# Order of the first loads and warm products at the start, and a router with tokens stationary on the turned residual stream

## The reference, cut to what matters

```python
hf = rms_norm(x, norm_ffn[layer])
...
logits = (h @ w_router).astype(jnp.float32) + b_router.astype(jnp.float32)
top_val, top_idx = lax.top_k(logits, TOP_K_EXPERTS)
top_w = jax.nn.softmax(top_val, axis=-1)
...
for e in range(N_EXPERTS):
    out = out + gates[..., e:e + 1] * swiglu(h, w_gu[e], w_down[e])
```

## Time and profile before

| | us |
|---|---|
| median of 3 runs (1910.8 to 1911.77) | 1911.51 |
| profiled execution | 1911.39 |
| its span | 1909.0 |
| TensorE busy | 1881.3 |
| VectorE, ScalarE busy | 1503.9, 1269.9 |

### The profile page before, as it was taken

One profiled execution on the slowest core, in us unless ns is written; L12 is line 12 of the kernel. 1 busy time (PEld: TensorE's weight loads), 2 busy tenths in 40 slices (PEclk: granted clock), 3 DMA queues, 4 the chain that ended last, 5 costly groups with the idle time before them and its releaser, 6 DMA issues.

```text
span 1909.0 us, 27543 instructions
## 1 busy us (share of the span) xinstructions
PE 1881.3 (99%) x9439; PEld 1581.3 (83%) x9439; DVE 1503.9 (79%) x1670; ACT 1269.9 (67%) x1689; POOL 86.6 (5%) x125
## 2 busy tenths in 40 slices
PE   7999999999999999999999999999999999999998
PEld 6887898888888887898788888888888888888886
DVE  4888664645456898665699999999999999999998
ACT  5747543544444747554578888888888788887885
POOL 1020000000000020001220000000000000000000
PEclk9999999999999999999999999999999999999999
DMA  9454653765554453564399999999999999999995
GB/s 341 136 187 133 213 188 132 260 204 194 196 176 139 132 189 123 193 215 137 115 394 404 382 395 352 409 380 371 392 357 407 376 375 384 364 406 377 377 406 199
DMA packets 182590, 530.17 MB, mean 278 GB/s; under 512 B 8896, under 2 KB 18176, under 8 KB 182256
## 3 DMA queue, kind: packets, MB, share of 16 engines
q1 hardware_dynamic: 175136, 503.38, 71.8%
q0 software_dynamic: 4368, 16.69, 2.4%
q10 hardware_dynamic: 3008, 9.07, 1.2%
HBM read 517.56 MB, written 11.56 MB: 277 GB/s over the span
## 4 chain that ended last, share of the span: by engine, by line
PE 91%; DVE 4%; ACT 2%; DMA 1%; issue 1%; POOL 0%; ACTq 0%; DVEq 0%; POOLq 0%; SPq 0%
PE bank L954 16%; PE bank L941 15%; PE bank L942 15%; PE bank L1957 7%; PE bank L1973 7%; PE bank L1965 7%; PE bank L1996 5%; PE bank L731 4%; PE bank L718 4%; PE bank L727 4%; PE bank L2026 2%; PE bank L992 1%; PE bank L2072 1%; DVE wlo L549 1%; DMA raw<-in_moe_w_gu 1%
## 5 line engine op out<-in xcount | busy, mean ns | idle before, releaser
L549 DVE TENSOR_TENSOR wlo<-raw,whi 128x1024 fp32r<-128x1024 f32 (+3 forms) x958 | 1133.8, 1218 | 194.0 <-ACT whi L546 164.0
L546 ACT ACTIVATE whi<-raw 128x1024 fp32r<-128x1024 f32 (+3 forms) x958 | 994.8, 1058 | 279.9 <-PE bank L954 143.8
L941 PE MATMUL bank<-whi,xg_hi 128*128 128x512 f32 x864 | 339.2, 393 | 0.0
L942 PE MATMUL bank<-whi,xg_lo 128*128 128x512 f32 x864 | 336.8, 390 | 0.0
L954 PE MATMUL bank<-wlo,xg_hi 128*128 128x512 f32 x896 | 276.9, 390 | 0.1
L954 PEld LDWEIGHTS bank<-wlo,xg_hi 128*128 128x128 f32 x896 | 168.7, 188 | 36.1 <-DVE wlo L549 0.5
L941 PEld LDWEIGHTS bank<-whi,xg_hi 128*128 128x128 f32 x864 | 162.7, 188 | 33.3 <-ACT whi L546 0.3
L942 PEld LDWEIGHTS bank<-whi,xg_lo 128*128 128x128 f32 x864 | 162.5, 188 | 33.0
L941 PE MATMUL bank<-whi,hidTw_hi 128*128 128x512 f32 x448 | 175.1, 391 | 0.0
L942 PE MATMUL bank<-whi,hidTw_lo 128*128 128x512 f32 x448 | 174.4, 389 | 0.0
L954 PE MATMUL bank<-wlo,hidTw_hi 128*128 128x512 f32 x448 | 138.2, 390 | 0.1
(11 more groups left out here) (353 smaller groups left out, 2028.7 us busy)
## 6 DMA issues: line engine op xcount, KB each, us to landing
raw<-in_moe_w_gu SPq DMA_DIRECT2D x224, 1024.0 KB, 7.4
raw<-in_moe_w_down SPq DMA_DIRECT2D x112, 1024.0 KB, 7.5
raw<-in_w_in SPq DMA_DIRECT2D x33, 1024.0 KB, 5.0
raw<-in_ffn_w_gu SPq DMA_DIRECT2D x28, 1024.0 KB, 5.2
raw<-in_xa_wkv SPq DMA_DIRECT2D x16, 1024.0 KB, 5.1
raw<-in_ffn_w_down SPq DMA_DIRECT2D x14, 1024.0 KB, 4.9
raw<-in_w_branch SPq DMA_DIRECT2D x12, 1024.0 KB, 5.1
raw<-in_w_out SPq DMA_DIRECT2D x8, 1024.0 KB, 5.2
```

Of the source, the lines that this page charges most:

```text
L546: self.eng.activation(whi[:, ps, 0:size], src, ACT.Copy).then_inc(high_ready, mark(high_ready, "high", p))
L549: self.eng.tensor_tensor(wlo[:, ps, 0:size], src, whi[:, ps, 0:size].bitcast(F32), ALU.subtract).then_inc(low_ready, mark(low_ready, "low" ...
L941: pe.matmul(bank[b][:, :], hi[:, k, 0:P], wh, start=first, stop=False)
L942: pe.matmul(bank[b][:, :], lo[:, k, 0:P], wh, start=False, stop=False)
```

## The change

**Start.** xT's three parts go to SyncE's queue, between the halves of unit 0: xT 0, half 0, xT 1, half 1, xT 2; x and the constants follow unit 1 instead of unit 2. The sinks' broadcast goes from GpSimd to ScalarE's queue, behind the gain columns, table, one-hot and identity; then ScalarE makes a dummy copy. TensorE begins with 14 products of a 128x128 tile of ones. The bias product stands behind PA's second piece, the wait for the identity behind PA's first block; the 12 transposes are gone.

**Router.** The router's weights are multiplied by the gain (VectorE), and TensorE turns x itself, in layer 1. The tokens are stationary now: 32 products, each of a chunk of `hT_hi` or `hT_lo` with 16 moving columns, the high and low parts of the weights side by side; sums for tile t stand in bank t, tokens on partitions. Copy and turning of logits are gone; `route` adds both halves of a bank. Four groups come in another order, one of them split wholly by VectorE. GpSimd multiplies the second half of x by the gain into `h`. The chosen are written as fp32r; places are two products with copies of triangle and ones in fp32r, and counts two more, into bank 7. `keep_busy` has 10 transposes ahead of the places and 5 behind the counts, where it had 8 ahead. The gather takes all high parts before the low ones, for both banks. VectorE's two `split_h` stand behind `pick`, and gates and ranks behind the third piece.

```diff
-        r_hi = place("r_hi", [P, KD, E], F32R, offset=region + 29 * K1 + 256)
-        r_lo = place("r_lo", [P, KD, E], F32R, offset=region + 29 * K1 + 512)
+        r_both = place("r_both", [P, KD, 2 * E], F32R, offset=region + 29 * K1 + 256)
+        r_hi, r_lo = r_both[:, :, 0:E], r_both[:, :, E:2 * E]
+        chosen_two = place("chosen_two", [P, NT, E], F32R, offset=region + 30 * K1 + 64)
         r_bias = place("r_bias", [P, E], offset=region + 29 * K1 + 768)
-        logits_T = place("logits_T", [E, S], offset=region + 35 * K1)
+        before_ones = place("before_ones", [P, 2 * P], F32R, offset=region + 35 * K1)
...
-            for n_, b in enumerate(ROWS):
+            for b in ROWS:
...
-                for low in range(2):
-                    for t in range(NT):
...
+            for low in range(2):
+                for t in range(NT):
+                    if low:
+                        pe.wait_ge(norm_ready, at("h_lo", t))
+                    else:
+                        pe.wait_ge(high_copied, at("h_hi", t))
+                    src = h_lo[:, t] if low else h_hi[t]
+                    for n_, b in enumerate(ROWS):
                         for i in range(4):
                             k = 4 * n_ + i
-                            src = h_lo[:, t] if low else h_hi[t]
                             ins = pe.matmul(bank[b][:, i * P:(i + 1) * P], src[:, k * P:(k + 1) * P], pick[:, t, :],
                                             start=not low and t == 0 and i == 0, stop=bool(low) and t == NT - 1 and i == 3)
-                ins.then_inc(gather_full, mark(gather_full, g, "gather", "first", n_))
+                        if low and t == NT - 1:
+                            ins.then_inc(gather_full, mark(gather_full, g, "gather", "first", n_))
...
-                if q == 0:
-                    low_gathered(g, "first")
+                if q < 2:
+                    low_gathered(g, "first", (q,))
...
-            nothing_yet(dve, "experts")
-            dve.wait_ge(bank_full[7], at("logits_turned"))
...
-                dve.scalar_tensor_tensor(rt[:, 0, t], bank[7][:, t * E:(t + 1) * E], rstd(1, "ffn", t), r_bias[:, :],
-                                         ALU.mult, ALU.add).then_inc(*((dve_freed[7], mark(dve_freed[7], "logits")) if t else
-                                                                       (vector_step, mark(vector_step))))
-            dve.wait_ge(dve_freed[7], at("logits"))
+                dve.wait_ge(bank_full[t], at("router", t))
+                dve.scalar_tensor_tensor(rt[:, 1, t], bank[t][:, 0:E], rstd(1, "ffn", t), r_bias[:, :], ALU.mult,
+                                         ALU.add).then_inc(vector_step, mark(vector_step))
+                dve.wait_ge(vector_step, tally.total[vector_step])
+                dve.scalar_tensor_tensor(rt[:, 0, t], bank[t][:, E:2 * E], rstd(1, "ffn", t), rt[:, 1, t], ALU.mult,
+                                         ALU.add).then_inc(dve_freed[t], mark(dve_freed[t], "logits", t))
+                dve.wait_ge(dve_freed[t], at("logits", t))
...
-            dve.tensor_scalar(rt[:, 5], rt[:, 1], 0.5 * TAKEN, None, ALU.is_lt).then_inc(choice_ready, mark(choice_ready, "chosen"))
+            dve.tensor_scalar(chosen_two[:, :, :], rt[:, 1], 0.5 * TAKEN, None, ALU.is_lt).then_inc(choice_ready, mark(choice_ready, "chosen"))
             dve.wait_ge(choice_ready, at("chosen"))
-            step(dve.tensor_scalar(rt[:, 9], rt[:, 5], -4096.0, 4096.0, ALU.mult, ALU.add))
-            split_h(dve, 1)
...
+                        sp.dma_start(xT[:, 0:2, :], a["xT"][:, 0:2, :]).then_inc(xT_loaded[0], mark(xT_loaded[0], "xT", 0, by=16))
                         sp.dma_start(raw[:, 0, 0:PIECE].rearrange("p (k n) -> p k n", k=2), view[:, 0:2]).then_inc(
                             raw_loaded[0], mark(raw_loaded[0], "raw", 0, by=16))
+                        sp.dma_start(xT[:, 2:4, :], a["xT"][:, 2:4, :]).then_inc(xT_loaded[1], mark(xT_loaded[1], "xT", 1, by=16))
                         sp.dma_start(raw[:, 0, PIECE:].rearrange("p (k n) -> p k n", k=2), view[:, 2:4]).then_inc(
                             rest_loaded, mark(rest_loaded, "rest of raw 0", by=16))
+                        sp.dma_start(xT[:, 4:8, :], a["xT"][:, 4:8, :]).then_inc(xT_loaded[2], mark(xT_loaded[2], "xT", 2, by=16))
                     else:
                         load_unit(sp, n, view, ku * width)
                     n += 1
-                    if n == 3:
+                    if n == 2:
                         sp.dma_start(x[:, :, :], a["x"].rearrange("b (t p) d -> p (b t) d", p=P)).then_inc(
...
+                if l:
+                    pool.wait_ge(gain_loaded[0], at(l, "ffn", "gain"))
+                    for t in range(NT):
+                        pool.wait_ge(dve_freed[lin_bank(l, "XO", 1, t)], at("merge", l, "XO", 1, t))
+                        pool.tensor_tensor(h[:, t, 512:], x[:, t, 512:], gain[0][:, 512:], ALU.mult).then_inc(
+                            late_h, mark(late_h, l, "ffn", "late h", t))
...
-            act.dma_start(xT[:, 2:4, :], a["xT"][:, 2:4, :]).then_inc(xT_loaded[1], mark(xT_loaded[1], "xT", 1, by=16))
-            act.dma_start(xT[:, 4:8, :], a["xT"][:, 4:8, :]).then_inc(xT_loaded[2], mark(xT_loaded[2], "xT", 2, by=16))
+            act.dma_start(sinks[:, :, 0, :], a["sinks"].partition_broadcast(P)).then_inc(
+                sinks_loaded, mark(sinks_loaded, "sinks", by=16))
+            act.wait_ge(pool_step, at("half"))
+            act.activation(stats[:, 94:95], stats[:, 95:96], ACT.Copy).then_inc(exp_ready, mark(exp_ready, "first table"))
...
-                    act.wait_ge(router_loaded, at("r_b"))
-                    act.activation(r_hi[:, :, :], r_raw[:, :, :], ACT.Copy).then_inc(high_copied, mark(high_copied, "r_hi"))
+                    act.wait_ge(router_scaled, at("r_w by gain"))
+                    act.activation(r_hi, r_raw[:, :, :], ACT.Copy).then_inc(high_copied, mark(high_copied, "r_hi"))
...
+                if l:
+                    act.wait_ge(consts_loaded, at("consts"))
+                    act.activation(before_ones[:, :], cst[:, C_TRI:C_TRI + 2 * P], ACT.Copy).then_inc(
+                        before_ready, mark(before_ready, "before and ones"))
...
-                to_high(l, "T3", hT_hi, (1,))
+                    to_high(l, "T3", hT_hi, (1,))
+                else:
+                    transposed_high((l, "T3", 1, 1), hT_hi, 4, 1, 7)
                 if l:
                     def high_of_h(t):
+                        act.wait_ge(norm_ready, at(l, "ffn", "h", 0, t))
+                        act.wait_ge(late_h, at(l, "ffn", "late h", t))
...
-            pe.wait_ge(table_loaded, at("onehot"))
-            fill(pe, 4, "act")
-            pe.matmul(bank[4][0:16, 0:384], table_sb[:, :], onehot_sb[:, :], start=True,
-                      stop=True).then_inc(bank_full[4], mark(bank_full[4], "bias_vec"))
-            pe.wait_ge(ident_loaded, at("ident"))
...
+            def bias_product():
+                pe.wait_ge(table_loaded, at("onehot"))
+                fill(pe, 4, "act")
+                pe.matmul(bank[4][0:16, 0:384], table_sb[:, :], onehot_sb[:, :], start=True,
+                          stop=True).then_inc(bank_full[4], mark(bank_full[4], "bias_vec"))
+
+            pe.wait_ge(warm_ready, at("warm"))
+            for _ in range(14):
+                pe.matmul(bank[5][:, 0:P], warm[:, :], warm[:, :], start=True, stop=True)
 
             for l in range(DEPTH):
                 if l == 0:
-                    keep_busy(pe, 5, 12)
-                    linear(l, "PA", 0, hT_hi, hT_lo, "xT")
+                    linear(l, "PA", 0, hT_hi, hT_lo, "xT", last=2)
+                    bias_product()
+                    linear(l, "PA", 0, hT_hi, hT_lo, "xT", first=2)
+                    pe.wait_ge(ident_loaded, at("ident"))
...
-                turn_all(l, "T3", h, norm_ready, lambda q, t: (l, "ffn", "h", q, t), (0,))
+                def turn_x(q, t):
+                    pe.wait_ge(dve_freed[lin_bank(l, "XO", q, t)], at("merge", l, "XO", q, t))
+                    turn([(x[:, t, (4 * q + i) * P:(4 * q + i + 1) * P], P, i * P) for i in range(4)], 4 + 2 * t + q, "dve", l, "T3", t, q)
+
+                if l:
+                    for t in range(NT):
+                        turn_x(0, t)
+                else:
+                    turn_all(l, "T3", h, norm_ready, lambda q, t: (l, "ffn", "h", q, t), (0,))
...
-                    def router(hi, lo, k, st, en):
-                        return pe.matmul(bank[0][0:E, 0:S], hi[:, k], lo[:, k], start=st, stop=en)
+                    def router(t, q, of):
+                        for k in range(4 * q, 4 * q + 4):
+                            ins = pe.matmul(bank[t][:, 0:2 * E], of[:, k, t * P:(t + 1) * P], r_both[:, k, :],
+                                            start=of is hT_hi and k == 0, stop=of is hT_lo and k == KD - 1)
+                        return ins
...
```

(76 more changed lines are left out.)

58 lines of the change are left out of this document (20 added, 38 removed).

## The result

| | before | after |
|---|---|---|
| median, us | 1910.80 (8 runs, 1910.15 to 1911.77) | 1916.39 (8 runs, 1914.09 to 1918.31) |
| profiled execution, span | 1911.39, 1909.0 | 1916.1, 1914.4 |
| ratio, with its interval | | 1.0028 [1.0018, 1.0038] |

The change made the kernel 0.28% slower. The forecast was 1902.0, between 1898.5 and 1907.0, with a chance of 0.03 for slower; the time lies outside the range and on the other side of no change.

The account below looks back on a forecast made before the run. TensorE, busy 1881.3 of 1909.0 us, was taken to bound the kernel. Start 7.2 plus router 2.3 made 9.5 us: 1901.9 by the profiled execution, 1902.0 for the median, range 1898.5 to 1907.0.

Parts of the forecast that it names:

- With VectorE's gates moved to before piece 3's remainder, the fourth piece ends at 951.4: First expert pieces after the router: fourth piece ends at 951.4 instead of 954.9, 3.5 us earlier if the clock stays high.
- so the gain holds to the end: Expert stage: the weight stream restarts earlier by as much as TensorE's work, so the full 9.5 us gain remains.
- The start: Loads and PA's first pieces: 6.75 us earlier first product, plus 1.18 for clock, less 0.7 for bias: 7.2 us gained.
- 7.2 us, if the feeding holds: Start: the 7.2 us gain requires loads and splits to arrive in time; tightest cover 0.1 us, at unit 2.
- Rival C: Start: late loads, ScalarE issuing or means cap its gain at 3.0 us; with router 2.3, 1906.2 us; chance 0.13.
- The 1.18 us for the clock: PA's first piece: 14 warm-up products raise the clock before the data, recovering 1.18 us of half-speed running.
- The router: Router, gather and first expert pieces: 2.3 us gained, with bounds from 1 us lost to 4.5 us gained.
- The low stretch: Router and gather: TensorE's reduced-clock period, forecast to last at most 7 us.
- E: Router into expert stage: early, lasting 1.2 GHz clock makes the kernel slower; 30 us of it gives 1913.6; chance 0.03.
- D: First softmax: late bias tables or mem give back the start's gain; router gains 2; total 1909.5 us; chance 0.07.
- The prediction's price for a stall: TensorE: a microsecond counts when it stands idle, or runs slowly, ahead of work it is otherwise ready for.

Follow-up runs that it names:

- rows one block of columns later: The changed kernel with ScalarE's `load_rows` moved from the second to the third block of columns of each trip: 1902.71 us, ratio 0.9958 to the kernel before.
- the start alone: The kernel before with only the change's loads, warm products and bias product; router, gather and order of gates as before: 1905.58 us, ratio 0.9977.

## Why the prediction was wrong

**The failing step.** It stands in the router's part: "With VectorE's gates moved to before piece 3's remainder, the fourth piece ends at 951.4". I priced the moved gates as VectorE's time ahead of one remainder, and never asked who waits for the gates themselves. GpSimd does, with 31 dependent small instructions and four scatters, and ScalarE's load of rows waits for these, with the split of all later weights behind it. The step costs 13.0 us alone (the kernel before with only that move), and taking away its consequence gives 13.7 back (rows one block of columns later). The sentence that followed from it, "so the gain holds to the end", is the one that the traces refute: all 8.2 us were in hand at 946.6, and lost at 991.

Two things were in the trace of before and not read: that the load of rows had a cover of only 7.0 us, of which a gain on TensorE's path takes its own size away if the chain doesn't move with it (in the start alone it did); and that `find_rows` already took 1.1 us for steps beside a remainder. With both, and with the chain's start of 943.7 that only the trace after shows, the step's price follows: nearly all of 31 steps at one per `wlo`, near 30 us, then 5 us to the last scatter and 10 to 11 us of landing, ends near 989 to 990 against a ScalarE that comes at 977.

**The start**, forecast -7.2: the sum into x is 5.43 us earlier, and the start alone gained 5.2. The mechanism held: first product at 7.12 (forecast 7.65), full speed at once, bias product 0.81. (Speed is read from the length of the products here. The granted clock of the kernel before stands at 1.00 over 14.40 to 18.30, where four products took 2.05 us; the column doesn't show that low stretch.) The term that was mis-sized is the feeding: "7.2 us, if the feeding holds". From the first piece to the fifth it takes 20.76 - 7.12 = 13.6 us, where four pieces of 2.72 and 0.7 of bias make 11.6: 2.1 us more, 0.5 of them offset by the earlier first product. The trace lists 1.1 of the 2.1 as idle time of TensorE (0.17, 0.41 and 0.53). ScalarE waits for weights' DMA 1.30, 0.97, 1.21 and 0.70 us. Rival C had this cap, with a gain of 3; the truth lies between. The 1.18 us for the clock were counted as if nothing stood behind the first piece; without warm-up they were all but free.

**The router**, forecast -2.3, was right in sum, in part by luck: places 2.1 us earlier beyond the start (forecast 2.7), first expert product 2.1 (forecast 2.8), end of the fourth piece 2.8 (2.3 taken); -2.2 by the difference of medians. The low stretch was 3.41 us, from 932.0 to 935.4, and lay ahead of the gather. I had left the place open and bounded it by 7 us. In other executions of kernels with the same router it was 0, 6.8 and 17.1 us.

**The rivals.** E had the sign but another cause: 26 us of low clock in the router. The low clock did add 2.9 us, yet behind the stall and as its consequence. D, a gain given back by something later, was right in kind, but placed at the first softmax. None named the chain from the gates over GpSimd to ScalarE.

**What stays open.** What decides how long the clock stays low in the router (0 to 17.1 us): the executions near 1907 of kernels with a median near 1903 had 17.1 in both profiles that I have of such. What the gap near 7 us of the earlier trace rows costs: 0.8 us in one pair of traces, 0.7 between medians that five runs don't separate. How much of the lost 13 us is the chain's later start and how much its slower pace. And the 2.1 us in the start: no run separated the order of the loads from their bandwidth.

## What to carry to other kernels

When an instruction is moved back, follow its result through every engine to the next wait that stands in a busy engine's stream, not only the time that it takes where it stood and where it goes. A wait that a trace doesn't list may be one that is just covered: compute its cover (here 7.0 us) before counting a gain on the other side, for an earlier consumer and a later producer both draw on it. And a chain of small GpSimd instructions has two prices, 0.22 to 0.29 us a step beside a VectorE at rest or reading PSUM, 1.1 us beside one that subtracts two SBUF tiles; beside an unbroken run of `scalar_tensor_tensor` of two SBUF tiles it stood still.

## What the runs showed of the hardware that I had not expected

- GpSimd's 128x16 instruction takes as long as the VectorE subtraction beside it where that reads two SBUF tiles: 1.15 us for 0.29. Beside 18 `scalar_tensor_tensor` in a row (1.14 us each) one such instruction took 19.29 us, the whole rest of the run.
- A single stall of TensorE (980.28 to 991.02) brought the granted clock to 0.50, over 983.2 to 996.85, so it cost a quarter more than its own length: 13.6 us for 10.7. The prediction's price for a stall would have left that out.
- An indirect scatter's data landed 7.9 to 10.4 us after its issue began in the kernel after, and 8.4 to 11.0 in the kernel before; the median load of 1 MB of expert weights (`w_gu`) took 7.3.
- The granted clock stood at 1.00 over the first pieces of the kernel before (14.40 to 18.30) and of the one with a single warm product (7 to 12 us), although their first four products took 2.05 and 2.07 us, against 1.07 later.
